# Hybrid decoder step: w_out in hi/lo products, output projection, norm and routing as one stage, one-hot rows for the first item

## The chip, the cores and the metric

The kernel runs on one core of a Trainium2 chip. The metric is the device time of one execution in microseconds; less is better. The profiler gives one execution with the times of every instruction, counted from the start of its span.

## The reference

One layer of a decoder is computed for 512 prompt tokens and 64 sample tokens (T = 576), of width 1024. Two branches (a Mamba-2 scan and a latent attention) are merged; what follows is the part that the change touches:

```
merged = sigmoid(g_a) * y_a + sigmoid(g_b) * y_b
out = merged @ p['w_out']
...
h = layer_norm(ALPHA * u + out)
logits = (h @ router_w + router_b)            # 32 experts
top_v, top_i = lax.top_k(logits, 4)
gate = softmax(top_v)
# each token's row goes to its 4 experts:
gu = xb @ w_gu[e] + b_gu[e]                   # (1024, 2048)
hidden = (clip(u) + 1.0) * (g * sigmoid(1.702 * g))
y = hidden @ w_dn[e] + b_dn[e]                # (1024, 1024)
out = layer_norm(ALPHA * h + sum over k of gate_k * y_k)
```

All is float32. Each expert's weights are 12 MB, and all 32 are read.

## The kernel before

The program is a row of stages. Each has its own block for every engine, its own semaphores, and ends in a barrier of all engines. The last four are the merge of branch a, `stage_out`, `stage_route` and `stage_experts_combine`. Tokens lie in NT = 5 tiles of 128 rows (the last has 64). KD = 8 is the number of 128-wide pieces of the width.

`stage_out` loads w_out (4 MB), the residual rows and the norm's gains, and multiplies in plain float32: for each tile 2 halves of 512 columns times 8 pieces (L1610), 80 matmuls; the profile has two records for each plain float32 matmul, so 160. VectorE (DVE) adds the residual and takes the statistics tile by tile (L1624 to L1634), then takes one root for all tiles, and only then scales all tiles (L1643 to L1647). SP stores the rows to `h_rows` in DRAM.

`stage_route` turns the rows on the tensor engine (PE, L1762), multiplies them by the router's weights (L1769), picks the four experts of a token on DVE (L1811 to L1834), counts with matmuls by a triangle of ones where in its expert's list each token stands (L1776 to L1779), and makes slot numbers and gates (L1847 to L1858). Then GpSimd (POOL) scatters 20 times 128 pairs of 8 bytes (token, row of the result) to the table `slots` in DRAM (L1750); when all have landed, SP and ScalarE (ACT) read the table back to `tok`: one transfer for the 32 experts and 18 for possible overflow items, 9 on each queue, each with its address loaded from SBUF (L1724, L1728, L1798). Meanwhile SP has loaded the first four weight slots of expert 0 (L1719).

`stage_experts_combine` works in items, one for each expert (E = 32) and more only where an expert has over 128 tokens. An item has NW = 12 weight slots of 1 MB, 8 for the gate and up matrix and 4 for the down matrix. A slot is loaded by SP to one of NRAW = 8 raw buffers (L1961), ACT rounds it to float32r (`w_hi`, L2123), DVE subtracts to get the rest (`w_lo`, L2172), and PE makes three products, hi times hi, hi times lo and lo times hi (`products`, L2044): 12 matmuls of 512 columns for a slot. `w_hi` and `w_lo` have four buffers (NHI). SP issues the load of a slot when the low part of the slot 8 before it is done (`wait_low`). POOL gathers the next item's rows of `h_rows` by an indirect DMA (L2002), copies the expert's column for the bias (L2006) and scatters the item's result to `y_rows` (L2016). PE turns the gathered rows in the middle of the down products (L2038, 8 turns for the rows, after 4 for the hidden part). Ahead of the first item there is a start: the gather of item 0's rows, four high and four low parts, the turns.

Each engine's instructions run in the order in which they are written for that engine; the only other order is by the semaphores.

## Time and profile before

| | us |
|---|---|
| median of 3 runs | 2855.95 (2853.38 to 2858.27) |
| the profiled execution | 2858.25 |
| its span | 2856.5 |
| granted tensor clock, mean | 0.935 |
| end of the last work of branch a's merge (DVE) | 1433.2 |
| first product with w_out | 1447.3 |
| first product of item 0 | 1641.6 |
| PE busy in all | 2562.5 (90%) |
| DVE busy in all | 1801.7 (63%) |

A row of the timeline reads: start, duration, engine, line, operation, what is written <- what is read, how many (xN), and in brackets how long the engine was idle before it and who ended that. The duration of a merged row runs from its first start to its last end. PE is the matmul, PEld the weight load that lies beside it, SPq, ACTq and POOLq are the engines' issuing sides.

### The profile page before, as it was taken

The numbers are of one execution on the slowest core, as the hardware profiler recorded it, in microseconds if no ns is written. First come the engines' busy times: TensorE is split into PE (matmuls) and PEld (weight loads), VectorE is DVE, ScalarE is ACT, GpSimd is POOL, SyncE is SP. The second block draws the span as 40 slices with busy tenths as digits, with TensorE's granted clock in tenths as the row PEclk, the third lists the DMA queues.
The fourth block names the chain that finished last, engine by engine and source line by source line (L and its number), as shares of the span: only waits on it lengthen the run. The fifth ranks groups of instructions, "written<-read, shape, count | busy, mean of one in ns | idle before, by whom it ended". The sixth has DMA issues, their size and how long they took to land. (4 is left out here: it accounts for less than half of the span.)

```text
span 2856.5 us, 35192 instructions
## 1 busy us (share of the span) xinstructions
PE 2562.5 (90%) x12631; PEld 1912.8 (67%) x12631; DVE 1801.7 (63%) x2118; ACT 1344.1 (47%) x1396; POOL 472.1 (17%) x333
## 2 busy tenths in 40 slices
PE   8697999698996999979976199999999999999996
PEld 5355555498994444548834188888888888888882
DVE  0343444333775666631013489999999999999996
ACT  0242322132324445420001177777777777777771
POOL 0002122000002233300001412222222222222220
PEclk9798999798998999979986599999999999999998
DMA  3103344132214313232123199999999999999995
GB/s 88 62 1 131 123 157 163 34 89 65 89 45 141 120 56 98 69 107 67 37 107 108 24 410 399 381 381 380 380 381 379 381 380 381 382 379 378 380 342 188
DMA packets 247096, 590.05 MB, mean 207 GB/s; under 512 B 28064, under 2 KB 117344, under 8 KB 242528
## 3 DMA queue, kind: packets, MB, share of 16 engines
q1 hardware_dynamic: 228392, 512.16, 49.6%
q0 software_dynamic: 17312, 76.57, 7.2%
q8 instruction: 64, 1.05, 0.2%
q14 instruction: 32, 0.26, 0.0%
q10 hardware_dynamic: 1296, 0.01, 0.0%
HBM read 555.78 MB, written 32.78 MB: 206 GB/s over the span
## 5 line engine op out<-in xcount | busy, mean ns | idle before, releaser
L2172 DVE TENSOR_TENSOR w_lo<-w_raw,w_hi 128x2048 fp32r<-128x2048 f32 x290 | 660.6, 2296 | 67.0 <-ACT w_hi L2123 66.6
L2123 ACT ACTIVATE w_hi<-w_raw 128x2048 fp32r<-128x2048 f32 x290 | 554.2, 1916 | 108.7 <-PE banks L2044 108.5
L2044 PE MATMUL banks<-w_hi,x_hi 128*128 128x512 f32 x1024 | 319.3, 393 | 5.1 <-DVE x_lo L2176 5.1
L2044 PE MATMUL banks<-w_hi,x_lo 128*128 128x512 f32 x1024 | 316.4, 390 | 0.0
L2044 PE MATMUL banks<-w_lo,x_hi 128*128 128x512 f32 x1024 | 316.0, 390 | 0.0
L2172 DVE TENSOR_TENSOR w_lo<-mergedT,w_hi 128x2048 fp32r<-128x2048 f32 x98 | 223.6, 2288 | 45.9 <-ACT w_hi L2123 45.9
L2123 ACT ACTIVATE w_hi<-mergedT 128x2048 fp32r<-128x2048 f32 x98 | 187.6, 1915 | 97.7 <-SPq L1971 62.7
L2044 PEld LDWEIGHTS banks<-w_lo,x_hi 128*128 128x128 f32 x1024 | 192.5, 188 | 40.6
L2044 PEld LDWEIGHTS banks<-w_hi,x_lo 128*128 128x128 f32 x1024 | 192.5, 188 | 40.4
L2044 PEld LDWEIGHTS banks<-w_hi,x_hi 128*128 128x128 f32 x1024 | 190.3, 188 | 43.4 <-issue 5.5
L2016 POOL DMA_INDIRECT y_rows<-xT,to_row x33 | 50.6, 1533 | 866.1 <-ACT xT L2153 865.8
L2044 PE MATMUL banks<-w_hi,h_lo 128*128 128x512 f32 x512 | 158.2, 390 | 0.0
L2044 PE MATMUL banks<-w_lo,h_hi 128*128 128x512 f32 x512 | 158.0, 390 | 0.0
L2044 PE MATMUL banks<-w_hi,h_hi 128*128 128x512 f32 x512 | 158.0, 390 | 0.0
L1306 PE MATMUL banks<-wz,xT 128*128 128x512 f32 (+1 forms) x320 | 145.1, 607 | 1.0 <-ACT zs L1421 1.0
L912 PE MATMUL banks_a<-xbcT,w_br_a 128*128 128x288 f32 x512 | 125.5, 406 | 0.0
L2038 PE MATMUL banks<-const,xT 128*128 128x128 f32 x520 | 68.3, 275 | 57.8 <-DMA xT<-h_rows,from_row 57.8
L912 PEld LDWEIGHTS banks_a<-xbcT,w_br_a 128*128 128x128 f32 x512 | 96.8, 190 | 26.1
L2044 PEld LDWEIGHTS banks<-w_hi,h_hi 128*128 128x128 f32 x512 | 96.1, 188 | 20.6
L2044 PEld LDWEIGHTS banks<-w_hi,h_lo 128*128 128x128 f32 x512 | 96.1, 188 | 20.3
L2044 PEld LDWEIGHTS banks<-w_lo,h_hi 128*128 128x128 f32 x512 | 96.1, 188 | 20.3
L1306 PEld LDWEIGHTS banks<-wz,xT 128*128 128x128 f32 (+1 forms) x320 | 57.6, 185 | 74.7 <-issue 74.3
(416 smaller groups left out, 4500.8 us busy)
## 6 DMA issues: line engine op xcount, KB each, us to landing
w_raw<-in_exp_w_gu SPq DMA_DIRECT2D x194, 1024.0 KB, 7.7
w_raw<-in_exp_w_down SPq DMA_DIRECT2D x96, 1024.0 KB, 8.2
mergedT<-in_exp_w_gu SPq DMA_DIRECT2D x66, 1024.0 KB, 8.4
mergedT<-in_exp_w_down SPq DMA_DIRECT2D x32, 1024.0 KB, 5.5
w_x<-in_w_in SPq DMA_DIRECT2D x12, 1024.0 KB
out<-h SPq DMA_DIRECT2D x20, 512.0 KB, 2.6
wz<-in_w_in SPq DMA_DIRECT2D x4, 2048.0 KB
dec<-acs_rows SPq DMA_DIRECT2D x16, 512.0 KB, 3.9
```

What stands on the lines that cost most here:

```text
L912: mm = pe.matmul(banks[:, b + 2 + piece, 0:H2], w_br[:, m % 2, k, :], x_of(k)[:, piece * H2:(piece + 1) * H2], start=(k == 0), stop=(k == ...
L1306: mm = pe.matmul(banks[0:n, 7, :], sb.xT[:, q, P * i:P * i + n], wz[:, g % 2, q, :], start=(q == 0), stop=(q == KD - 1))
L2016: pool.indirect_dma_start(out=io.y_rows, out_offset=bass.IndirectOffsetOnAxis(ap=to_row[:, par, :].bitcast(U32), axis=0), in_=y_out, in_of ...
L2038: mm = pe.transpose(banks[:, TURN_BANK[unit], k * P:(k + 1) * P], src[:, (k0 + k) * P:(k0 + k + 1) * P], K[:, K_ID:K_ID + P])
L2044: mm = pe.matmul(banks[:, bank + c, :], x[:, k, :], part[:, s % NHI, j, c * 512:(c + 1) * 512], start=start, stop=last)
L2123: act.activation(w_hi[:, s % NHI], raw(s, par), ACT.Copy).then_inc(hi_ready, 1)
L2172: dve.tensor_tensor(w_lo[:, s % NHI], raw(s, par), w_hi[:, s % NHI].bitcast(F32), ALU.subtract).then_inc(lo_ready, 1)
```

## The change

`stage_out` and `stage_route` become one stage, `stage_choose`, and some of the routing's DMA work moves into the experts' stage. Constants and buffers follow (`w_hi`, `w_lo`, `x_hi`, `x_lo`, `h_hi`, `h_lo` and `pair` now live across both stages; the raw buffers 0 to 5 are the separate ones and 6 and 7 the room of `mergedT`).

- w_out is loaded in four quarters, each split by ACT and DVE as an expert's slot is, and so is each tile of the merged input. PE makes three products for each pair: 5 tiles x 8 pieces x 3 x 2 halves = 240 matmuls.
- Each tile is normed in full before the next; PE turns tile i - 1 and makes its logits between the products of tile i.
- The ranks need 5 matmuls in place of 15, the counts 5 small ones with experts on the partitions; the list of overflow items comes from small matmuls in place of scans on one partition.
- For the first LISTED = 3 experts DVE makes one-hot tiles (`spot`). With those of expert 0 PE multiplies the rows themselves (40 plain float32 matmuls of 128 columns), which gives item 0's rows already turned. `tok` of the experts 0 to 2 comes from 15 matmuls of 2 columns.
- Slots 0 to 3 of expert 0 are split to their high parts within the stage, slot 0 to its low part too.
- The 20 scatters, the table's read and the 18 reads for overflow items move to the experts' stage: POOL scatters after it has issued the gather of item 1; SP reads the table after the loads of items 0 and 1, all 19 transfers on its own queue; POOL waits for them before the loop over the items from 2 on.

```diff
-            def _(pe):
-                pe.wait_ge(w_in_, 32)
-                for i in range(NT):
...
-                        for k in range(KD):
-                            mm = pe.matmul(banks[0:n, 2 * (i % 4) + c, :], sb.mergedT[:, k, P * i:P * i + n], w[:, c, k, :],
-                                           start=(k == 0), stop=(k == KD - 1))
...
+                for q in range(4):
+                    sp.dma_start(w_raw[q], io.wo[2 * P * q:2 * P * (q + 1), :].rearrange("(c p) n -> p c n", p=P)).then_inc(w_in_[q], 16)
...
                 for s in range(AHEAD):
-                    sp.dma_start(sb.w_raw[s], weight_slot(io, 0, s)).then_inc(first_in, 16)
-
-                sp.wait_ge(scattered, 16 * NT * TOPK)
...
+                    sp.wait_ge(wo_low, s + 1)
+                    sp.dma_start(w_raw[s], weight_slot(io, 0, s)).then_inc(first_in[s], 16)
...
+                def mix(i, q):
+                    n = ROWS[i]
+                    hi, lo = part_of(i)
+                    for j in range(2):
+                        k = 2 * q + j
+                        for x, part in ((hi, w_hi), (hi, w_lo), (lo, w_hi)):
+                            for c in range(2):
+                                mm = pe.matmul(banks[0:n, 2 * (i % 2) + c, :], x[:, k, 0:n], part[:, q, j, c * 512:(c + 1) * 512],
...
+                for i in range(NT):
+                    pe.wait_ge(m_low, i + 1)
+                    if i >= 2:
+                        pe.wait_ge(summed, i - 1)
+                    for q in range(4):
+                        if i == 0:
+                            pe.wait_ge(wo_low, q + 1)
+                        mm = mix(i, q)
+                        if q == 3:
+                            mm.then_inc(mixed, 1)
+                        if q == 2 and i >= 1:
+                            turn(i - 1)
...
+                    if i >= 1:
+                        logits(i - 1)
+                turn(NT - 1)
+                logits(NT - 1)
...
+                pe.wait_ge(spotted, 1)
+                for k in range(KD):
+                    for i in range(NT):
+                        n = ROWS[i]
+                        mm = pe.matmul(banks[:, k // 4, (k % 4) * P:(k % 4 + 1) * P], h[0:n, i, k * P:(k + 1) * P], spots[0:n, 0, i, :],
+                                       start=(i == 0), stop=(i == NT - 1))
...
+                pe.wait_ge(spotted, LISTED)
+                for e in range(LISTED):
+                    for i in range(NT):
+                        n = ROWS[i]
+                        mm = pe.matmul(banks[:, 2, 2 * e:2 * e + 2], spots[0:n, e, i, :], vals[0:n, i, e, :], start=(i == 0), stop=(i == NT - 1))
+                mm.then_inc(told, 1)
...
                 for s in range(AHEAD):
                     sp.sem_inc(w_in_[s], 16)
-                sp.wait_ge(x_in, 16)
-                n_more = items(sp, run)
+                run(0, 0)
+                run(1, 1)
+                sp.wait_ge(scattered, 16 * NT * TOPK)
+                with nc.allow_non_contiguous_dma(reason="a table of 8-byte pairs"):
+                    sp.dma_start(sb.tok[:, LISTED:E, :], io.slots.rearrange("(e c) a -> c e a", c=CAP)[0:P, LISTED:E]).then_inc(tabled, 16)
+                for q in range(NOVF + 1):
+                    at = sp.value_load(sb.item_slot[0:1, q:q + 1], min_val=0, max_val=E * CAP - P)
+                    sp.dma_start(sb.tok[:, E + q, :], io.slots[bass.ds(at, P), :]).then_inc(tabled, 16)
+                n_more = items(sp, run, 1)
...
-                gather(0, 0)
                 choose(0, 0)
                 pool.tensor_copy(to_row[:, 1, :], K[:, K_PAIR:K_PAIR + 1]).then_inc(to_put, 1)
                 pool.wait_ge(to_put, 1)
                 send(1)
-                n = items(pool, run)
+                e_next = expert(pool, 1)
+                gather(1, 1)
+                choose(e_next, 1)
+                for i in range(NT):
+                    n = ROWS[i]
+                    for k in range(TOPK):
+                        pool.indirect_dma_start(out=io.slots, out_offset=bass.IndirectOffsetOnAxis(ap=sb.slot[0:n, i, k:k + 1].bitcast(U32), axis=0),
+                                                in_=sb.pair[0:n, i * TOPK + k, :], in_offset=None).then_inc(scattered, 16)
+                scatter(0, 0)
+                run(1, 1)
+                pool.wait_ge(tabled, 16 * (NOVF + 2))
+                n = items(pool, run, 1)
```

On POOL, from the end of the routing into the items, this stood in a row before (`ISA` rows are register and semaphore work; x20 are the scatters):

```order
L1743 TENSOR_TENSOR b_all<-xT,b_all 32x3072
L1750 DMA slots<-pair,slot 20480x2 x20
L1707 UNCONDITIONAL_BRANCH
L140 ISA
L1994 UNCONDITIONAL_BRANCH
L1997 COPY from_row<-tok 128x1
L2002 DMA xT<-h_rows,from_row 128x1024
L2006 CAST pick<-const 128x128
L2027 CAST to_row<-const 128x1
L2016 DMA y_rows<-xT,to_row 2305x1024
```

and this stands there now (the changed kernel's own line numbers: L2129 is the scatter of pairs, L2096 the gather of rows, L2110 the scatter of results):

```order
L2120 CAST to_row<-const 128x1
L2110 DMA y_rows<-xT,to_row 2305x1024
L2038 TENSOR_LOAD item_expert
L2038 ISA x2
L2092 COPY from_row<-tok 128x1
L2096 DMA xT<-h_rows,from_row 128x1024
L2100 ISA
L2100 COPY pick<-const 128x128
L2129 DMA slots<-pair,slot 20480x2 x20
L2103 COPY to_row<-tok 128x1
L2110 DMA y_rows<-xT,to_row 2305x1024
L2038 TENSOR_LOAD item_expert
```

The gather of item 0's rows is gone, that of item 1's rows stands ahead of the 20 scatters, and item 0's result and the gather of item 2's rows (the next L2096) stand behind them.

On PE, between the last logits and the first product of item 0, this stood before (L1776 and L1777 are the ranks, L1779 the counts):

```order
L1769 MATMUL banks<-wr,hT 64x32 x8
L1777 MATMUL banks<-sel,const 128x32
...
L1779 MATMUL banks<-sel,const 128x32 x5
L1707 UNCONDITIONAL_BRANCH
L2033 UNCONDITIONAL_BRANCH
L2038 MATMUL banks<-const,xT 128x128 x8
L1931 UNCONDITIONAL_BRANCH
```

and this stands there now (L1731 and L1733 are the ranks, L1736 the counts, L1743 the rows of item 0 by one-hot tiles, L1756 the list of overflow items, L1762 the `tok` of three experts):

```order
L1708 MATMUL banks<-wr,mergedT 64x32 x8
L1731 MATMUL banks<-mergedT,const 128x160
...
L1733 MATMUL banks<-mergedT,const 128x32
L1736 MATMUL banks<-const,mergedT 32x2 x5
L1743 MATMUL banks<-w_raw,h 128x128 x15
L1749 MATMUL banks<-over,const 32x2
L1750 MATMUL banks<-over,const 1x2
L1743 MATMUL banks<-w_raw,h 128x128 x20
L1756 MATMUL banks<-xT,const 1x18 x8
L1743 MATMUL banks<-w_raw,h 128x128 x5
L1762 MATMUL banks<-vals,w_raw 128x2 x15
```

The one-hot products take the place of the turns of gathered rows, and stand ahead of the barrier between the stages.

## Rows read from the trace of the kernel before

**Rows 1.** Busy time by stretch, from the end of branch a's merge to item 0.

```profile
core 0: us, PE busy (x) PEld busy (x) DVE busy (x) ACT busy (x) POOL busy (x), PEclk, DMA share, GB/s
1434.00:1447.30 13.30, 0.04 (x1) 0.04 (x1) 0.07 (x1) 1.25 (x1) 0.00 (x0) 0.59 0.95 343
1447.30:1519.40 72.10, 72.10 (x160) 29.61 (x160) 11.12 (x20) 0.00 (x0) 0.00 (x0) 0.96 0.12 43
1519.40:1585.30 65.90, 28.95 (x160) 28.22 (x160) 32.87 (x89) 9.81 (x14) 12.99 (x5) 0.54 0.34 116
1585.30:1629.20 43.90, 0.00 (x0) 0.00 (x0) 13.43 (x10) 0.00 (x0) 23.13 (x21) 0.50 0.09 2
1629.20:1641.60 12.40, 1.97 (x8) 1.57 (x8) 10.19 (x6) 8.28 (x6) 10.37 (x7) 0.50 0.44 113
```

**Rows 2.** Transfers from 1434 to 1642: GB/s in 40 slices of 5.2 us.

```profile
GB/s 267 389 402 329 79 0 0 0 0 0 0 0 3 2 0 0 0 36 165 192 60 131 332 406 154 0 0 0 0 0 1 1 1 1 0 8 3 0 101 181
```

**Rows 3.** The chain of work that ended last: pieces of items 0 and 1.

```profile
1641.64 12.53 PE banks L2044 x48
...
1670.55 1.31 PE banks L2038 x12
...
1672.33 17.71 PE banks L2044 x78
...
1706.41 1.31 PE banks L2038 x12
```

**Rows 4.** Busy time by stretch: the first products of item 0.

```profile
1641.60:1644.40 2.80, 2.76 (x7) 2.21 (x8) 0.00 (x0) 0.46 (x1) 0.98 (x3) 0.50 0.92 354
```

**Rows 5.** Timeline: plain float32 matmul records of 32 and 128 columns.

```profile
30.28 1.92 PE L239 MATMUL banks<-w_dt,xT 128*128 128x32 f32 x16
...
246.91 1.06 PE L430 MATMUL banks<-probT,val 128*128 128x128 f32 x8
...
1550.24 13.74 PE L1769 MATMUL banks<-wr,hT 128*128 128x32 f32 x80
```

**Rows 6.** Timeline of DVE: the norm, then the choice of experts.

```profile
1519.43 1.28 DVE L1624 SCALAR_TENSOR_TENSOR h<-x_tok,banks 64x512 f32<-64x512 f32 x2 [11.03 <-PE banks L1610]
...
1522.96 0.81 DVE L1643 TENSOR_SCALAR h<-h,mv 128x1024 f32<-128x1024 f32 x1
...
1538.02 1.22 DVE L1647 TENSOR_TENSOR h<-h,b_b 64x1024 f32<-64x1024 f32 x1
...
1564.13 0.57 DVE L1816 TENSOR_TENSOR lg<-banks,br 128x32 f32<-128x32 f32 x5 [20.89 <-PE banks L1769]
...
1568.53 0.09 DVE L1834 MEMSET sel<- 64x32 f32 x1
```

**Rows 7.** Costliest groups of the page: a slot's low and high part.

```profile
L2172 DVE TENSOR_TENSOR w_lo<-w_raw,w_hi 128x2048 fp32r<-128x2048 f32 x290 | 660.6, 2296 | 67.0 <-ACT w_hi L2123 66.6
L2123 ACT ACTIVATE w_hi<-w_raw 128x2048 fp32r<-128x2048 f32 x290 | 554.2, 1916 | 108.7 <-PE banks L2044 108.5
```

**Rows 8.** Timeline: scatters of pairs on POOL beside work of DVE.

```profile
1588.23 2.55 DVE L1869 TENSOR_TENSOR found<-match,code 1x2304 f32<-1x2304 f32 x1
1589.35 2.27 POOL L1750 DMA_INDIRECT slots<-pair,slot  x1 [0.30 <-issue]
1590.82 2.54 DVE L1870 TENSOR_REDUCE listed<-found 1x18 f32<-1x2304 f32 x1
1591.93 0.96 POOL L1750 DMA_INDIRECT slots<-pair,slot  x1 [0.30 <-issue]
```

**Rows 9.** Timeline: a gather of rows on POOL in an item.

```profile
1687.09 2.67 POOL L2002 DMA_INDIRECT xT<-h_rows,from_row  x1 [0.89 <-POOL from_row L1997]
```

**Rows 10.** Indirect transfers of the items, 1650 to 2750: time to landing.

```profile
DMA to landing us min/median/max: 7.7/8.7/9.6
```

**Rows 11.** Timeline: half of the reads for overflow items, on SP's queue.

```profile
1616.85 10.03 SPq L1728 DMA_DIRECT2D tok<-slots  x9
```

**Rows 12.** Busy time by stretch: the transfers in items 0 and 1.

```profile
1650.00:1700.00 50.00, 50.00 (x232) 41.52 (x231) 46.14 (x32) 38.09 (x28) 8.24 (x5) 1.00 1.03 410
```

More of the change, by code:

```diff
@@ L1927, in wait_low, with items @@
             eng.wait_ge(lo_ready, it * NW + (NW + s + 1))
[L1929 to L1931 removed]
+        def items(eng, body, first=0):
+            with eng.Fori(first, E // 2) as i:
                 body(i * 2, 0)
```

529 lines of the change are left out of this document (287 added, 242 removed).

## The prediction

> **What bounds the kernel now.** I read the chain of waits first. From item 0 on it is the tensor engine (PE) without a break: products of one item after the other, 35.86 us an item (the turns of gathered rows start at 1670.55 in item 0 and at 1706.41 in item 1), 17.71 us for 78 products, so 0.227 us for one of 512 columns [rows 3]. The page's share (PE 90% busy) is thus an average of two things. The 32 items are bound by PE, and the change alters nothing within a steady item. The 207.6 us between branch a's merge and item 0 are bound by waits: read by stretch, PE works 103 of them [rows 1]. It waits 13.3 us for w_out, has 72.1 us of products, then 65.9 us in which norm, turns, router and choice follow each other with 29 us of PE work, then 43.9 us with none (20 scatters, then the table's read), then 12.4 us of start for item 0. The question is when item 0's first product comes (1641.64 before), and what the work moved into the items costs them.
>
> **w_out.** Removed: 80 plain float32 matmuls, 72.1 us at a mean granted clock of 0.96 [rows 1]. Added: 240 products at 0.227, 54.5 us with the clock high. They start when the first quarter is there and split. The slices give 267 GB/s for the first 5.2 us, then some 390 [rows 2]: 1.05 MB by 4.3 us at the earliest, if the quarters land one by one; if they land together it is 13.3. I take 1440. The split is an expert slot's: high part 1.92, low part 2.29 [rows 7], so PE starts at 1444.3. The four quarters and two tiles of the input need 4 x 2.29 and about 2 x 1.2 of DVE (half a slot each, an estimate), 11.6 us from 1441.9, so the last low part ends at 1453.5. PE's first products are at the low clock, 0.50 granted (1.2 GHz), 0.40 us each [rows 4]. The old stage had a mean of 0.96 over 72.1 us [rows 1], which is 5.8 us at 0.5 and the rest at 1; I take the same 5.6 us, 14 low products and 34 high ones: 1444.3 + 5.6 + 7.7 = 1457.6. Take 1458 for the end of tile 0, 1455 to 1461 as bounds.
>
> **Tiles 1 to 4.** 4 x 48 x 0.227 = 43.6. Turns: the chain's piece of 12 takes 1.31 [rows 3], so 8 take 0.87, four times 3.5. Logits: 16 records of 32 columns take about 1.76 us at the high clock (to the next row's start; the row says 1.92) [rows 5], three times 5.3. A tile's PE work is then 13.6 us, and a tile's norm on DVE is 3.5 to the scaling [rows 6] and 3.3 for the scaling (1522.96 to 1539.2 for five tiles), 6.8, plus 1.2 for the next tile's low part. So the norm of tile i ends ahead of the turn that PE makes 8.2 us after it; it hides behind the products, and would cost 1 us for each 1 us by which it passed 8.2. With 0.3 for each small wait: 1458 + 43.6 + 3.5 + 5.3 + 1.1 = 1511.5. The last tile has no cover: norm 6.8, 8 turns and the copies about 1.3, 16 logit records at the low clock 0.17 each (13.74 for 80) [rows 5] 2.7. Logits are there at 1522.3, where before it was 1564.1.
>
> **Choice, ranks, one-hot.** From the first add to the selection 4.5 us [rows 6], now 4.7: 1527.0. Ranks: 480 columns in all; plain float32 of 512 columns takes 72.1 / 80 = 0.9 at the high level, so 480 at the low one 1.7, with loads 2.0. Two copies and five one-hot tiles, 1.4: 1530.4. The rows of item 0 are 40 plain matmuls of 128 columns, 80 records. The nearest row has 8 in 1.06, 0.113 apart at the high level [rows 5], so 9.0; at the low level twice as much, 18. PE did almost nothing from 1518 on, so it starts low, and these matmuls are dense, so I expect the high level after some 5 us: 11.5. Small matmuls between them 1, then 30 records of the token table at 0.11 to 0.17 [rows 5], 4.2, and 0.4 for DVE's last copies: 1547.6. DVE's own list (overflow list, slots, gates, low part of the rows) is some 14 us from 1533 by the old stage's ops of 0.3 and ends about then. Barrier about 0.9, and PE's first instruction 0.3 later: **first product at 1548.8**, 92.8 us earlier. Gone with it are the 20 scatters, the table's read and item 0's gather, parts and turns, that is the whole 43.9 and 12.4 us of waiting [rows 1]; late next is the chain above.
>
> **What moves into the items.** Call the stage's start S. PE starts at S + 0.3, so it reaches the turns of item 2's rows (in item 1) 64.8 us later by the old distance 1706.41 - 1641.64 [rows 3]: S + 65. *POOL*: bias column, the dummy result and the gather of item 1 keep it to about S + 10.5. Then come the 20 scatters, and behind them in its queue item 0's result and the gather of item 2. A scatter takes 0.96 beside a reduction of DVE and 2.27 beside a subtraction or product of two tiles, where it ends with DVE's instruction plus 0.9 [rows 8]; a gather in an item takes 2.67 [rows 9]. With 0.3 between, 20 take 25 us with DVE idle and 59 us at 2.97 each. DVE has 12 long subtractions in 35.86 us and shorter work between, so I take 2.3: S + 56.5. Item 0's result and the next gather need some 7 more, landing 8.7 [rows 10]: item 2's rows land near S + 71, 6 us late. At 1.27 a scatter it would be S + 51, no wait; at 2.97, S + 85, 20 late.
>
> The Trainium skill (GPSIMD Engine Reference, Key points) says that GpSimd shares its SBUF interfaces with VectorE and contends with DVE instructions that have two SBUF inputs. By that rule every scatter behind a low part is slow and the sum has its loss; if it did not hold in an item, the result would be that of rival A. This trace agrees: 2.27 against 0.96 us.
>
> *SP*: the loads of item 2's slots 4 to 11 stand behind the wait for the scatters and 19 table transfers. Nine took 10.03 [rows 11], so the 19 take about 21 us. SP can reach the wait when the low part of item 1's slot 7 is done, S + 56; the scatters have landed at about S + 60. The queue is free at S + 82, the load lands 5 to 8 us later, its parts need 4.2 [rows 7]: ready at S + 92 to 94. PE needs that slot (number 28) at S + 3.6 + 28 x 2.99 = S + 87.3, or S + 93.3 after the 6 us already lost. So the two waits overlap, and the second adds 0 to 1. The pause is survivable since eight buffers and the backlog carry PE; afterwards transfers run at 410 GB/s [rows 12] against the 380 that 13.6 MB in 35.86 us need, so the lead returns. An idle PE restarts at the low clock, 0.50 granted [rows 4], some 1 us more. Sum: **7 us lost** once, bounds 0 and 25. One more place is tight: slot 4 is issued at S + 0.3, lands by S + 8 if it takes the 7.7 of [rows 10], and is split by S + 13.5, with a table load on ACT; PE needs it at S + 15.6. I count this as nothing lost; if it lands 3 us later it costs 1.
>
> **Sum.** 2856.5 - 92.8 + 7 = 2770.7 of span. The profiled execution has 1.75 us outside its span and is 2.3 above the median, so 2770.7 + 1.75 - 2.3 = 2770.
>
> **Rivals.** *A, no loss in the items*: scatters near 1.3 us, or the gather lands in time. For it: short work of DVE leaves gaps. Against it: rows 8 and 9. 2763. *B, a long loss in items 1 and 2*: scatters near 3 us, so that SP starts its table reads at S + 75 and slot 28 is ready at S + 109, 22 late, or the small transfers wait behind the weights' backlog. For it: the gather's 2.67 and a queue that is full. 2780 to 2800. *C, the new stage is longer*: quarters that land together (PE starts at 1451, 7 later), the one-hot products low all through (7 more), the norm past its cover. 2771 to 2785. *D, slower than before*: item 2's rows come so late behind the scatters on POOL that the loss passes the 92.8 us. Rows land at about S + 10.5 + 20 t + 14; against S + 65 this is a loss of 20 t - 40, so t must pass 6.6 us a scatter. The longest here is 2.67, so it needs small indirect transfers that block POOL behind the weights, which only an item's load would show. At t = 7 it gives 2863. *E, the products gain nothing*: if PE stayed at the low clock in the mixed stream of tiles, the 192 products of tiles 1 to 4 cost 0.40 and 33 us more: 2803. Against it: 0.96 granted in the old products [rows 1]; the short logits between should not undo it.
>
> **How the numbers follow.** Forecast 0.45, A 0.15, B 0.20, C 0.13, E 0.04, D 0.02, the stage shorter than I sum 0.01. The predicted time is the forecast's, 2770. Below, A with a stage 8 us shorter gives 2755; above, B and C up to 2792; what lies outside is most of E, D and the far end of B. Measurement can tell about 0.2% (6 us) from no change. Every case but D and a bit of its neighbourhood ends faster by more: faster 0.97, same 0.01, slower 0.02.
>
> **What would show it.** In the changed profile: the first w_out product between 1442 and 1447; the tiles' products 0.227 each at a granted clock near 1; PE idle for under 1 us at each turn; logits complete near 1522; the first product of item 0 near 1549; items of 35.86 us but for one; 20 scatters in about 46 us, each ending just after a low part; a PE wait for gathered rows in item 1 of some 6 us; SP's 19 reads near S + 60 to S + 82. It is wrong if item 0 starts past 1560, if PE waits again after item 2, or if a steady item is longer than 35.9 us.

## The result, and the profile after

| | before | after |
|---|---|---|
| median (lowest to highest) | 2854.66 us (2852.06 to 2858.27), 4 runs | 2806.22 us (2800.5 to 2809.62), 4 runs |
| profiled execution, span | 2856.5 us | 2801.1 us (2803.2 with what lies around it) |
| granted clock, mean | 0.935 | 0.945 |

The ratio is 0.983, 95% interval 0.9818 to 0.9842: 1.7% faster. The prediction of 2770 us, range 2755 to 2792, is 36 us too low, and the time lies above the range. Of these 36 us, 29 are in one term, the loss within the first items, and 2 in a first product of item 0 that comes later. The other 5 are between executions: the sum took the profiled one to be 2.3 us above the median, and it is 3.0 below.

Busy time by stretch of the changed kernel, the same columns as in [rows 1]: the wait for w_out, the five tiles, the rest of the routing stage, the 56 us from item 0's first product, and the gap in item 2.

```profile
1431.30:1441.30 10.00, 0.00 (x0) 0.00 (x0) 3.52 (x2) 4.75 (x3) 0.67 (x2) 0.66 0.82 314
1441.30:1510.40 69.10, 67.05 (x320) 53.57 (x321) 43.25 (x44) 16.66 (x21) 13.93 (x3) 0.95 0.49 172
1510.40:1550.50 40.10, 27.00 (x191) 24.02 (x189) 27.15 (x89) 11.09 (x11) 0.42 (x2) 0.70 0.03 7
1550.50:1606.50 56.00, 47.61 (x192) 37.85 (x193) 40.37 (x26) 31.36 (x23) 41.57 (x27) 0.91 0.96 300
1648.10:1668.80 20.70, 0.08 (x2) 0.04 (x1) 2.29 (x1) 4.95 (x3) 1.61 (x4) 0.62 0.57 193
```

The stage did what was said: 119 us from the merge's end to item 0, where it was 208 before, and PE (TensorE) starts item 0 at 1550.54 (forecast 1548.8). What went wrong is in the last two lines. In [rows 12] the weights move at 410 GB/s and PE is busy all the time; here the mean is 300 and PE is idle for 8.4 of 56 us, and it idles 20.6 us more in item 2.

The chain that ended last shows both places (start, us, what):

```profile
1556.34 27.85 DMA w_raw<-in_exp_w_down
1584.29 1.92 ACT w_hi L2225
...
1590.51 1.92 PE banks L2142 x12
...
1618.24 2.50 SPq L2064
...
1621.49 13.77 SPq L2067
...
1656.09 7.00 DMA w_raw<-in_exp_w_gu
1663.18 1.28 ACT L2225
1664.47 1.92 ACT w_hi L2225
1666.41 2.30 DVE w_lo L2272
1668.76 6.30 PE banks L2148 x17
```

In [rows 3] the same chain is PE alone. Here it leaves PE twice. First to a load of weights that took 27.85 us to land. Then to SP: L2064 is the read of the table, L2067 the 18 reads of the overflow lists; after them the next load of weights leaves at 1656.09, lands in 7.0 us, and needs ACT's function table (the load at L2225), the high part and the low part (5.5 us) before PE has a product again.

How much was lost is read from the turns of the gathered rows, L2142 x12, against item 0's first product. Before, they stand 28.9 us behind it, and one item is 35.86 us [rows 3]. After, they stand at 39.97, 77.5 and 136.6 us. The excess, called the loss from here on, is 11.1 us in item 0, 12.7 by item 1 and 36.0 by item 2; from there on each item takes 35.86 again. The span adds up: 1550.54 + 36.0 + 1214.6 for the rest, and in the kernel before 1641.64 + 1214.9. Forecast was a loss of 7 where 36.0 came; the other steps of the span together are within 2 us. So the experiments ask what these 36.0 us are.

### The profile page after: what moved, and what is told of

The parts are those of the page before. It is cut to its first block and busy times, and to the rows that moved or that the text cites. A ratio compares the mean times of both kernels' runs of the same rounds, so it can differ in the third digit from the quotient of the medians.

```text
span 2801.1 us, 35520 instructions
## 1 busy us (share of the span) xinstructions
PE 2560.0 (91%) x12813; PEld 1931.8 (69%) x12813; DVE 1813.2 (65%) x2130; ACT 1358.1 (48%) x1409; POOL 474.1 (17%) x331
## 5 line engine op out<-in xcount | busy, mean ns | idle before, releaser
L2225 ACT ACTIVATE w_hi<-w_raw 128x2048 fp32r<-128x2048 f32 x288 | 550.4, 1916 | 113.5 <-PE banks L2148 104.0
L2148 PE MATMUL banks<-w_hi,x_hi 128*128 128x512 f32 x1024 | 321.2, 395 | 23.9 <-DVE w_lo L2272 21.6
L2225 ACT ACTIVATE w_hi<-mergedT 128x2048 fp32r<-128x2048 f32 x96 | 184.1, 1917 | 41.0 <-PE banks L2148 34.5
L2110 POOL DMA_INDIRECT y_rows<-xT,to_row x33 | 50.8, 1538 | 847.1 <-ACT xT L2255 846.7
L963 DVE TENSOR_TENSOR prod_a<-banks_a,sig_a 128x576 f32<-128x576 f32 x8 | 6.1, 757 | 154.2 <-PE banks_a L918 154.2
```

What stands on the lines that cost most here:

```text
L963: dve.tensor_tensor(o.rearrange("p (a n) -> p a n", a=2), banks[:, b + 2:b + 4, 0:H2], sig[:, m % 2, :].rearrange("p (a n) -> p a n", a=2) ...
L2110: pool.indirect_dma_start(out=io.y_rows, out_offset=bass.IndirectOffsetOnAxis(ap=to_row[:, par, :].bitcast(U32), axis=0), in_=y_out, in_of ...
L2148: mm = pe.matmul(banks[:, bank + c, :], x[:, k, :], part[:, s % NHI, j, c * 512:(c + 1) * 512], start=start, stop=last)
L2225: act.activation(w_hi[:, s % NHI], raw(s, par), ACT.Copy).then_inc(hi_ready, 1)
```

## The experiments

The first w_out product comes between 1436.6 and 1449.1 us, by differences in earlier stages that no edit touches. So the table has distances within one execution: the stage from the first w_out product to item 0's first product, and the loss up to the turns of items 0, 1, 2 and 3 (after item 3 it stays). In two places the turns of the rows themselves waited, e4 in item 3 and e11 in item 1; there the table has what was lost once they were through. The times, beside the kernel before on the same chip, are of one profiled execution each for e1 to e8. The four to five executions that e9, e10 and e11 have lie up to 17 us apart, so these single times are rough; the argument rests on the distances, and those are of one execution each too. The stage differs by up to 5 us between runs whose edits hardly touch it (107.8 in e7, 112.9 in e3), so a difference of that size in it proves nothing.

| run | stage | item 0 | 1 | 2 | 3 | time (before) |
|---|---|---|---|---|---|---|
| after | 109.2 | 11.1 | 12.7 | 36.0 | 36.0 | 2806.2 (2854.7) |
| e1 scatters early | 129.0 | 4.8 | 4.8 | 24.6 | 24.6 | 2808.2 (2855.3) |
| e2 half of them | 114.7 | 7.1 | 7.2 | 27.3 | 27.3 | 2799.7 (2855.3) |
| e3 place-first lists | 112.9 | 5.7 | 5.7 | 14.9 | 14.9 | 2790.9 (2855.3) |
| e4 reads on POOL | 110.2 | 9.3 | 12.0 | 12.0 | 21.6 | 2791.7 (2855.3) |
| e5 stride of 648 | 109.5 | 10.1 | 12.7 | 35.8 | 35.8 | 2811.4 (2860.9) |
| e6 slot 4 early | 110.3 | 4.5 | 11.9 | 35.2 | 35.2 | 2810.5 (2860.9) |
| e7 no list reads | 107.8 | 11.0 | 12.7 | 13.6 | 13.6 | 2783.7 (2860.9) |
| e8 plain products | 132.3 | 12.2 | 13.8 | 35.3 | 35.3 | 2824.1 (2860.9) |
| e9 = e3 + e7 | 109.5 | 6.2 | 6.2 | 6.2 | 6.2 | 2778.6 (2860.7) |
| e10 = e9 and three more | 109.7 | 2.5 | 2.5 | 2.5 | 2.5 | 2772.4 (2860.7) |
| e11 = e10 less one edit | 105.4 | 1.6 | 3.8 | 3.8 | 3.8 | 2775.0 (2863.3) |

### e1 and e2: the scatters out of item 0

```diff
                 pool.wait_ge(b_low, 2)
+                pool.wait_ge(noted, 2)
+                pool.wait_ge(cleared, 16)
+                for u in range(0, 20):
+                    i, k = divmod(u, TOPK)
+                    n = ROWS[i]
+                    pool.indirect_dma_start(out=io.slots, out_offset=bass.IndirectOffsetOnAxis(ap=sb.slot[0:n, i, k:k + 1].bitcast(U32), axis=0),
+                                            in_=sb.pair[0:n, i * TOPK + k, :], in_offset=None).then_inc(scattered, 16)
+                pool.wait_ge(scattered, 16 * 20)
```

This stands at the end of POOL's part of the routing stage, and the same 20 are gone from item 0. In e2 the range ends at 10.

> The 20 scatters of slot pairs are issued and waited for at the end of the routing stage, so the items hold none; nothing else is moved. The figure to read is the distance from item 0's first product to the turns of the gathered rows (39.97 us in the changed kernel, 28.91 in the kernel before), and the same to item 2's turns (136.6, before 100.6). Theory 1 (each scatter of 128 pairs of 8 bytes takes some 0.55 us of all 16 DMA engines from the weights, 11 us for 20): item 0 falls back to 29 to 31 us, and the weights move at 400 GB/s and more from 1.5 item-slots on. Rival 1 (item 0 is late because the loads of slots 4 and up start 6.5 us later against the products than before, and the scatters only pass through gaps): item 0 stays at 38 to 40. The loss around item 2 (25 us) should stay in both, 20 to 27 us, as SP's table reads are untouched. The whole kernel is not expected to gain: the routing stage grows by the 20 scatters, some 20 to 30 us, and at least 11 come back.

> Ten of the 20 scatters go to the end of the routing stage and are waited for there, ten stay in item 0. Theory 1 (0.55 us of transfer per scatter): item 0 takes 33 to 36 us to the turns, midway between 28.9 and 40. If there is a slack that the first scatters use up (the products are not waiting at first), it is nearer to 30. Rival 1 (late start of the loads): 38 to 40, as with all 20 or with none. Item 2's loss stays at 20 to 27 us.

Item 0 took 33.67 us to the turns with no scatter (a loss of 4.8), 36.05 with ten (7.1), 39.97 with twenty (11.1). Neither theory alone has it: the scatters are worth 6.3 us, and 4.8 are there without them. What these 4.8 are, ACT (ScalarE) shows in e1, by its timeline:

```profile
1574.14 1.28 ACT L2227 ACT_TABLE_LOAD   x1 [34.31 <-DMA w_raw<-in_exp_w_gu]
1575.44 1.92 ACT L2227 ACTIVATE w_hi<-w_raw 128x2048 fp32r<-128x2048 f32 x1
1578.73 1.92 ACT L2227 ACTIVATE w_hi<-w_raw 128x2048 fp32r<-128x2048 f32 x1 [1.38 <-DMA w_raw<-in_exp_w_gu]
1581.76 1.92 ACT L2227 ACTIVATE w_hi<-mergedT 128x2048 fp32r<-128x2048 f32 x1 [1.11 <-DMA mergedT<-in_exp_w_gu]
```

Each of the first high parts waits for its load. The loads of slots 4 and up leave 1.0 us after item 0's first product; in the kernel before they left at 1636.18, 5.5 us ahead of it, since its item 0 had its own rows to turn first. And they start slowly; why is not shown. GB/s in 40 slices of 1.4 us from the first product on, of before, after and e1:

```profile
GB/s 287 421 421 418 421 418 415 413 418 398 404 398 413 410 415 392 413 418 415 392 413 418 415 398 407 418 415 392 410 404 418 401 407 415 421 421 413 410 401 415
...
GB/s 12 76 234 222 170 395 421 418 424 408 417 226 64 123 255 411 411 298 120 381 405 99 296 387 296 279 155 281 396 416 413 184 252 401 323 284 401 407 418 421
...
GB/s 12 64 217 190 199 386 421 418 421 421 415 407 415 413 410 407 410 415 398 413 410 410 410 407 413 415 404 407 415 395 407 410 407 415 407 410 410 421 418 418
```

In after and e1 alike the first five slices have 12 to 234 GB/s. The holes (64, 120, 99, 155) are in after alone, while the scatters run, and in e1 they are gone.

### e3: another layout of the lists

```diff
-    c[:, K_BASE:K_BASE + E] = CAP * np.arange(E)
+    c[:, K_BASE:K_BASE + E] = np.arange(E)
-    dve.tensor_tensor(place, rank, K[:, K_BASE:K_BASE + E].unsqueeze(1).broadcast_to((P, NT, E)), ALU.add)
+    dve.scalar_tensor_tensor(out=place, in0=rank, scalar=float(E), in1=K[:, K_BASE:K_BASE + E].unsqueeze(1).broadcast_to((P, NT, E)), op0=ALU.mult, op1=ALU.add)
-    sp.dma_start(sb.tok[:, LISTED:E, :], io.slots.rearrange("(e c) a -> c e a", c=CAP)[0:P, LISTED:E])
+    sp.dma_start(sb.tok[:, LISTED:E, :], io.slots[0:E * P].rearrange("(c e) a -> c e a", e=E)[:, LISTED:E])
```

The overflow codes, and the reads that use them, follow the layout. So the edit changes three things at once: where the scatters write, the shape of the table's read, and the 18 reads, which now take every 32nd pair.

> The list in DRAM is laid out by place first and expert second, so that the table read takes 128 pieces of 232 bytes in place of 3712 pieces of 8 bytes; the 18 small reads stay with 128 pieces each. Theory 2 (the first small read's issue was blocked 13.8 us because the 3712 pieces stand behind the weights' backlog and fill the queue): the block is gone, all 18 reads go out at 1.1 us, SP's pause falls from 37.9 to 21 to 24 us, and the loss around item 2 from 25 to 8 to 12 us; the kernel is 13 to 17 us faster than the changed one, 2789 to 2793. Rival 2 (a small read's issue waits for the backlog of the weights whatever the table's shape): a block of 10 us or more remains, the pause is 32 or more, and the kernel gains 5 us at most.

SP's queue by its timeline, after first, then e3:

```profile
1618.24 2.50 SPq L2064 DMA_DIRECT2D tok<-slots  x1
1621.49 32.92 SPq L2067 DMA_DIRECT2D tok<-slots  x18
1656.09 1.06 SPq L2049 DMA_DIRECT2D w_raw<-in_exp_w_gu  x2
```

```profile
1618.40 0.47 SPq L2064 DMA_DIRECT2D tok<-slots  x1
1619.61 20.53 SPq L2068 DMA_DIRECT2D tok<-slots  x18
1641.82 1.06 SPq L2049 DMA_DIRECT2D w_raw<-in_exp_w_gu  x2
```

The backlog of weights is much the same in both, about 12 us at full rate, and SP comes to the table at about the same time. With 3712 pieces the first small read is held for 13.77 us; with 128 it is not, and SP's pause falls from 37.9 to 23.4 us, the loss after item 1 from 23.3 to 9.2. So the backlog alone does not block. Nor do the pieces alone: the kernel before read its whole table, 4096 pieces of 8 bytes, with no weights under way, and the reads behind it went out at 1.1 us each.

```profile
1615.37 0.37 SPq L1724 DMA_DIRECT2D tok<-slots  x1
1616.85 10.03 SPq L1728 DMA_DIRECT2D tok<-slots  x9
```

It takes both, many pieces behind a backlog. The Trainium skill (DMA: Bandwidth & Descriptors, Rules for kernel authors) says that a last dimension that is strided is lowered to one descriptor per element, and should be rearranged to be contiguous. The case here is a neighbour of that one, since the last dimension is a contiguous pair of 8 bytes in a strided list. No run shows the elements of a pair apart; what the runs show is the price at the next instruction of the queue.

What I had not expected is item 0: its loss fell to 5.7, though the same 20 scatters of 8-byte pairs run there. Packets of the 56 us from the first product, after and then e3:

```profile
DMA packets 4991, 16.80 MB, mean 300 GB/s; under 512 B 902, under 2 KB 902, under 8 KB 4987
...
DMA packets 5998, 20.68 MB, mean 369 GB/s; under 512 B 963, under 2 KB 963, under 8 KB 5994
```

The number of small packets is about the same (902 and 963), and the bytes, nearly all of them weights, are almost a quarter more. In this stretch neither kernel has read the table yet, so only the places of the scatters differ. So it is not the count of small writes that costs, but where they go.

### e4: the list reads on POOL

```diff
-                for q in range(NOVF + 1):
-                    at = sp.value_load(sb.item_slot[0:1, q:q + 1], min_val=0, max_val=E * CAP - P)
-                    sp.dma_start(sb.tok[:, E + q, :], io.slots[bass.ds(at, P), :]).then_inc(tabled, 16)
...
                 run(1, 1)
+                run(2, 0)
+                for q in range(NOVF + 1):
+                    at = pool.value_load(sb.item_slot[0:1, q:q + 1], min_val=0, max_val=E * CAP - P)
+                    pool.dma_start(sb.tok[:, E + q, :], io.slots[bass.ds(at, P), :]).then_inc(tabled_late, 16)
+                run(3, 1)
```

> SP does the table read alone; the 18 reads of the overflow lists go to POOL's queue, after item 2's result. Theory 2: the load that follows the table read on SP takes over the block of some 14 us, SP's pause is 14 to 18 us in place of 37.9, which the lead of the buffers covers but for 0 to 5 us; 20 to 25 us come back and the kernel is at 2781 to 2788. Rival 2b (it is the sum of the reads that matters, wherever they run: their 2304 pieces of 8 bytes cost the weights as the scatters do): some 10 us are lost again in item 2 or 3, and the gain is 12 to 16 us. Item 0 stays at 39 to 41 us in both.

The block moved to SP's loads, as theory 2 says: two loads take 13.05 us from 1622.40, and item 2 loses nothing. But item 3 lost 9.6 us, 8.2 of them without work and the rest at slower turns and products behind it. POOL (GpSimd) and PE by their timelines:

```profile
1679.87 1.30 POOL L2134 DMA_DIRECT2D tok<-slots  x2
...
1699.46 0.53 POOL L2134 DMA_DIRECT2D tok<-slots  x1 [0.61 <-issue]
```

```profile
1710.53 1.97 PE L2145 MATMUL banks<-const,xT 128*128 128x128 f32 x8 [8.16 <-DMA xT<-h_rows,from_row]
```

```profile
DMA packets 4703, 15.87 MB, mean 397 GB/s; under 512 B 835, under 2 KB 835, under 8 KB 4702
```

The last row is of 1675 to 1715: the weights were hardly slowed (a mean of 397 GB/s; 373 to 398 in most slices while the reads ran, 406 to 418 in most of those before and after), so rival 2b's mechanism is out too, although its size was near. The gather of item 4's rows stood behind 18 reads of 1.14 us in POOL's queue. It is the wait that the prediction put in item 1, for another instruction. These small reads take little from the stream, where the scattered small writes of the changed kernel took a fifth. But each of them reads 128 neighbouring pairs, so the comparison does not tell reads from writes.

### e5: a stride of 648 places

```diff
-CAP = 640
+CAP = 648
```

> The lists keep their expert-first layout, but an expert's part is 648 places long in place of 640, so the same 8-byte pairs go to addresses 5184 bytes apart in place of 5120. Theory 1a (the scatters are cheap when an address pattern suits the memory; 5120 bytes apart is a bad one): item 0 loses 5 to 7 us as with the place-first layout, in place of 9 to 11, and the weights' rate during the scatters stays near 370 GB/s. Rival 1b (what helped the place-first layout is that a scatter's 128 pairs fall into one stretch of 4 KB, not 32 stretches): item 0 loses 9 to 11 as in the changed kernel, at a mean near 300 GB/s. Item 2's loss stays at 22 to 26.

A loss of 10.1 in item 0, and a mean of 305 GB/s over the same 56 us:

```profile
DMA packets 5063, 17.07 MB, mean 305 GB/s; under 512 B 908, under 2 KB 908, under 8 KB 5059
```

The exact distance of the lists is not it. What is left is that the place-first layout puts a scatter's pairs into a few KB that lie together, and the expert-first one into 32 stretches. That this is the cause is an inference from two layouts; no run varied it in steps.

### e6: slot 4 loaded early

```diff
                     sp.dma_start(io.h_rows[P * i:P * i + ROWS[i], :], h[0:ROWS[i], i, :]).then_inc(stored, 16)
+                sp.dma_start(w_raw[4], weight_slot(io, 0, 4)).then_inc(early, 16)
...
-                run(0, 0)
+                run(0, 0, AHEAD + 1)
```

> The load of item 0's slot 4 is moved to the routing stage, behind the rows' stores, where its buffer is free once the gains are used; all else as in the changed kernel. By the late start of the loads (items begin with loads 1 us behind the first product, where before they began 5.5 us ahead), one slot fewer to fetch is 2.6 us at 400 GB/s, and the slow first 5 us of a restarted stream stay: item 0's loss goes from 9 to 11 down to 6.5 to 8.5 us. Rival (item 0 is set by the scatters alone, which hold back slots 8 to 11 whatever came first): no change, 9 to 11. Item 2's loss stays at 22 to 26.

Item 0's loss fell to 4.5, more than the load is worth, but item 1's grew to 7.4: 11.9 in all against 12.7. Neither expectation had this. PE waits only when the stream is behind; one slot fewer in item 0 puts off the debt that the scatters make, and does not remove it. With scatters that cost little it should come to its worth (e10, e11).

### e7: no list reads

```diff
+                n_reads = sp.value_load(sb.n_over[0:1, 0:1], min_val=0, max_val=NOVF)
+                with sp.If(0 < n_reads):
                     for q in range(NOVF + 1):
                         at = sp.value_load(sb.item_slot[0:1, q:q + 1], min_val=0, max_val=E * CAP - P)
                         sp.dma_start(sb.tok[:, E + q, :], io.slots[bass.ds(at, P), :]).then_inc(tabled, 16)
```

POOL waits for them under the same condition, and the places of absent items are filled with a valid row in the routing stage.

> The 18 reads of the overflow lists run only where an expert has more than 128 tokens, which none has in this data; so they are not executed. The table read of 3712 pieces stays. Theory 2 (the loss around item 2 is SP's pause, of it 14 us behind the backlog of weights and table pieces, 19 to 20 in 17 more reads): the first load after the table read is blocked 12 to 14 us, the pause is 14 to 17 in place of 37.9, and the loss from item 1 on falls from 25 to 2 to 5 us; unlike with the reads on POOL nothing is lost later. Whole kernel: 20 to 23 us faster than the changed one, 2782 to 2787. Rival (it is the block, not the reads, that starves the products): the loss stays over 12.

```profile
1619.64 1.70 SPq L2065 DMA_DIRECT2D tok<-slots  x1
1624.15 12.15 SPq L2050 DMA_DIRECT2D w_raw<-in_exp_w_gu  x2
1636.56 1.07 SPq L2050 DMA_DIRECT2D mergedT<-in_exp_w_gu  x2
```

```profile
1666.28 1.53 PE L2148 MATMUL banks<-const,xT 128*128 128x128 f32 x12 [0.76 <-DVE xT L2291]
```

The loads are blocked as in e4, yet item 2 loses only 0.9 us where it lost 23.3. The three pauses of SP stand in a row: 16.9 us cost 0.9 (the block alone), 23.4 cost 9.2 (the reads alone, e3), 37.9 cost 23.3 (both). The pause less its cost is 16.0, 14.2 and 14.6 us. So the buffers' lead covers some 14 to 16 us, and what a pause has beyond that is lost in full. The reads alone starve PE, the block alone all but doesn't, and together they cost more than the sum of the two.

### e8: plain products in the new stage

```diff
-                    hi, lo = part_of(i)
                     for j in range(2):
                         k = 2 * q + j
-                        for x, part in ((hi, w_hi), (hi, w_lo), (lo, w_hi)):
-                            for c in range(2):
-                                mm = pe.matmul(banks[0:n, 2 * (i % 2) + c, :], x[:, k, 0:n], part[:, q, j, c * 512:(c + 1) * 512],
-                                               start=(k == 0 and x is hi and part is w_hi), stop=(k == KD - 1 and x is lo))
+                        for c in range(2):
+                            mm = pe.matmul(banks[0:n, 2 * (i % 2) + c, :], sb.mergedT[:, k, P * i:P * i + n], w_raw[q][:, j, c * 512:(c + 1) * 512],
+                                           start=(k == 0), stop=(k == KD - 1))
...
-                    sp.wait_ge(wo_low, s + 1)
+                    sp.wait_ge(mixed, NT)
```

> In the new stage the products of w_out are plain float32, 80 matmuls as before, straight from the raw tiles; the splits on ScalarE and VectorE still run, unused, and item 0's first slots are loaded once the last tile is mixed. It tells what the hi/lo products are worth inside the new stage. By the prediction's terms (72.1 us for 80 plain products against 54.5 for 240 at 0.227, and the first 5 us at the low clock in both) the stage from the first w_out product to item 0's first product takes 15 to 20 us more than the changed kernel's 109.2, 124 to 129, since the norm stays hidden in both. Rival (with the longer products the norms, turns and clock losses between tiles shrink, or the tail hides part): 8 to 13 us more. The losses in items 0 and 2 stay.

```profile
1442.60:1523.70 81.10, 81.10 (x241) 38.41 (x241) 43.35 (x44) 16.57 (x21) 13.03 (x3) 0.96 0.22 68
1523.70:1574.90 51.20, 32.49 (x192) 28.80 (x191) 27.29 (x89) 11.09 (x11) 0.43 (x3) 0.60 0.35 129
```

The stage is 23.1 us longer, above both expectations: 12.0 in the tiles, 11.1 behind them. Of the 11.1, 5.6 are there before the last logits are read, and these are of my edit's making. The high part of the first expert's slot stands ahead of the last tile's root on ACT, and its load now leaves only after the last product:

```profile
L1775 ACT ACTIVATE w_hi<-w_raw 128x2048 fp32r<-128x2048 f32 x4 | 7.6, 1903 | 10.4 <-DMA w_raw<-in_exp_w_gu 10.4
```

The other 5.5 are PE's work, 32.5 us in place of 27.0 at a mean granted clock of 0.60 and not 0.70. So the hi/lo products are worth 12.0 us in the tiles, not the 17.6 (72.1 less 54.5) of bare products, and with them the loads are free to leave early. Some of the difference is tile 0's wait for its gains, which the longer products hide and the shorter ones don't: in e10, where the wait is gone, the tiles take 65.3 us, 15.8 less than here.

### e9, e10 and e11: versions that beat both

e9 has the layout of e3 and the condition of e7. e10 adds the early slot 4, and these two:

```diff
                 for i in range(NT):
-                    sp.dma_start(h[0:ROWS[i], i, :], token_dram(io.xp, io.xs, i)).then_inc(x_in, 16)
-                sp.dma_start(g_b, io.g1.broadcast_to((P, D))).then_inc(gb_in, 16)
-                sp.dma_start(b_b, io.b1.broadcast_to((P, D))).then_inc(gb_in, 16)
+                    sp.dma_start(h[0:ROWS[i], i, :], token_dram(io.xp, io.xs, i)).then_inc(x_in[i], 16)
+                    if i == 0:
+                        sp.dma_start(g_b, io.g1.broadcast_to((P, D))).then_inc(gb_in, 16)
+                        sp.dma_start(b_b, io.b1.broadcast_to((P, D))).then_inc(gb_in, 16)
...
+                for u in range(0, 8):
+                    i, k = divmod(u, TOPK)
+                    n = ROWS[i]
+                    pool.indirect_dma_start(out=io.slots, out_offset=bass.IndirectOffsetOnAxis(ap=sb.slot[0:n, i, k:k + 1].bitcast(U32), axis=0),
+                                            in_=sb.pair[0:n, i * TOPK + k, :], in_offset=None).then_inc(sb.scattered, 16)
```

The eight scatters stand where e1 has its 20, on a semaphore that both stages share, so that the routing stage doesn't wait for them. e11 leaves them out.

> The place-first layout of the lists (scatters into one stretch, table read of 128 pieces) together with the overflow reads that run only where there is overflow; none has it in this data, so they are not executed. If the two causes found add up, item 0 loses 5 to 6 us as in the run with the layout alone, item 1 nothing, and item 2 at most 1 us (9.2 with the layout and the reads, 0.9 with neither read nor layout): 5 to 7 us in all against 36 in the changed kernel, so 2775 to 2779. If instead the block of some 13 us at SP after the table read was the table's pieces and nothing else matters, it is the same figure; if the backlog of weights blocks SP anyway, a block stays at the next load but costs nothing, since the queue is then full of weights. A third loss at a new place (item 2 or 3, as with the reads on POOL) would show the sum is not what I think.

> As e9, and three more edits: slot 4 of item 0 is loaded in the routing stage; 8 of the 20 scatters are issued there while DVE still writes the gates and the one-hot products run (they are waited for with the others in item 1); and the gains and the first tile's input are fetched ahead of the other tiles' input, each tile waiting for its own, so that the norm of tile 0 does not wait 7.3 us. Theory: item 0 is short by its start of the loads and its 20 scatters; 2.6 us come from slot 4, 0 to 2 from the 8 scatters, so the loss is 1 to 4 us in place of 5 to 7. The routing stage is 1 to 4 us shorter by the norm of tile 0 and the clock it costs (2.0 us wait and one more stretch at the low clock). Together 2768 to 2775, ratio to the kernel before 0.970 to 0.973. Rival (the slow first 5 us of the stream after a pause is the whole of item 0's loss, whatever is to be fetched): loss 5 to 6, 2773 to 2778.

> As e10, with all 20 scatters in item 0 again; the layout, the reads only where there is overflow, the early slot 4 and the order of the gains stay. In e10 VectorE's last step of the routing stage came 4.1 us after the last product, while the early scatters ran, and item 0 lost 2.5 us. If the early scatters were what held up the end of the stage: the stage from the first w_out product to item 0's first product falls from 109.7 to 105 to 106 us, item 0's loss is 3 to 4 us, and the whole is 2766 to 2771 in fast chips, 2 to 4 us under e10. Rival (the delay in e10 was a chance of that execution, as no such delay stands in e1, which had scatters at the same place): the stage is 105 to 106 too, but the whole is not under e10's median, since only its profiled run was late and the 8 early scatters are worth 1 us.

| | median (lowest to highest), runs | ratio to before, 95% interval |
|---|---|---|
| e9 | 2778.62 (2771.13 to 2781.12), 4 | 0.972, 0.970 to 0.974 |
| e10 | 2772.4 (2770.15 to 2781.32), 5 | 0.9699, 0.9678 to 0.972 |
| e11 | 2775.01 (2770.19 to 2787.48), 4 | 0.971, 0.9685 to 0.9736 |

e9 is as expected: 6.2 us lost in item 0 and nothing later, so the two causes add up and no third place shows. e10 lost 2.5 us there, as expected. Its stage was not shorter, though. From the first w_out product to the last logits but one it took 65.3 us in place of 69.1, since the norm of tile 0 no longer waited for its gains, but the end came late. DVE (VectorE) in e10, then in e11:

```profile
1551.91 0.16 DVE L1972 CAST tok<-banks 128x3 int32<-128x3 f32 x1 [5.92 <-DMA dec<-acs_rows]
```

```profile
1546.34 0.16 DVE L1965 CAST tok<-banks 128x3 int32<-128x3 f32 x1 [2.85 <-PE banks L1766]
```

In e10 PE had finished 4.1 us before this copy; e11, without the early scatters, has no such delay, and its stage is 105.4. But e1 had scatters at the same place and its copy came at once, and e11's median is not under e10's. So what held that copy is open (the releaser named is a transfer of an earlier stage and can't be right). Against e9, the trace of e10 shows 3.7 us less loss, that of e11 2.4 us less loss and 4.0 us less stage; but the intervals of the three overlap, and the times do not tell them apart. All three are faster than both kernels.

In e11, slot 4 early and the place-first layout brought item 0's loss down to 1.6 us with all 20 scatters in it. Then PE was early enough to meet another wait, in item 1, for the gathered rows of item 2:

```profile
1617.62 1.09 PE L2152 MATMUL banks<-const,xT 128*128 128x128 f32 x8 [1.91 <-DMA xT<-h_rows,from_row]
```

POOL had issued that gather at 1608.72, behind the 20 scatters (1557.94 to 1602.45) and item 0's result.

## Why the prediction was wrong, point by point

**The new stage: right, in part by luck.** Terms and measured: first w_out product 1444.3 and 1441.3, end of tile 0 1458 and 1454, tiles' end 1511.5 and 1510.4, logits 1522.3 and 1520.5, start of the one-hot products 1530.4 and 1529.2, first product of item 0 1548.8 and 1550.54. Several errors nearly cancel. The first w_out product came 3.0 us earlier, 1.9 of them because the stage before ended earlier. The tiles then took 69.1 us and not 67.2, the one-hot products with the small ones between 14.7 and not 12.5, and what follows them 0.7 us more than taken. The restart at the low clock was foreseen, and it came again on the way. The norm of tile 0 waited for its gains (7.26 us, on DVE), which the prediction did not have. So PE waited 2.01 us for tile 0's rows, and then the granted clock fell to 0.50:

```profile
1456.64 1.22 DVE L1846 SCALAR_TENSOR_TENSOR h<-h,banks 128x1024 f32<-128x1024 f32 x1 [7.26 <-DMA w_raw<-in_ln_b]
...
1464.23 1.10 PE L1700 MATMUL banks<-const,h 128*128 128x128 f32 x8 [2.01 <-DVE h L1863]
...
1465.30:1468.50 3.20, 3.20 (x9) 2.46 (x8) 0.01 (x1) 0.71 (x2) 0.00 (x0) 0.50 1.02 408
```

**The scatters' interval: right in kind.** 20 in 37.8 us, one in 1.9 where 2.3 was taken: 0.96 us for some, 2.3 to 3.0 for others, as [rows 8] had it.

**The wait for item 2's rows: did not occur here.** The prediction took 6 us for the gather behind the scatters. The turns of that gather stand in item 1 without idle time:

```profile
1628.04 1.47 PE L2142 MATMUL banks<-const,xT 128*128 128x128 f32 x12
```

The scatters were done earlier than taken, and PE was late already by 11 us. The mechanism is real. In e11, where item 0 loses only 1.6 us, it stands at the place that the prediction named, with 1.91 us: the rows released PE 69.3 us after the stage's start, where 71 was taken. e4 has it in item 3, with 18 reads in place of 20 scatters, 8.16 us.

**"Slot 4 ... I count this as nothing lost": the first step that failed.** The load landed in 7.5 us, where 7.7 was taken, and the slot was ready 14.4 us after the stage's start. PE wanted it at 13.5 and waited 0.93 us. The prediction had this need at 15.6, too late by its own rows: the 48 products of slots 0 to 3 take 12.53 us [rows 3]. But slot 4 is the small part, and the term had no other. The slots behind it came slowly, at 12 to 234 GB/s for the first seven us, and then with holes. The loss is 4.8 us without any scatter (e1), 6.3 more with them. The sum had the indirect transfers as work of POOL alone. That small transfers and weights meet was named only in rivals B and D, as weights that hold up the small ones; here it is the small writes that hold up the weights. The row that spoke of the slow start was [rows 2]: in its last slice, when the items' loads have begun (they left at 1636.18), it has 181 GB/s. I used its first slice, 267, for w_out, and not its last one for item 0.

**SP's pause, 21 us: the term that was mis-sized most.** It was 37.9. The 18 reads took 1.09 us each as [rows 11] says, and SP reached the table at S + 68.0 in place of S + 60, by the loss of item 0. The other 14 are the block of the first small read. The prediction priced 19 transfers by nine that ran with nothing else in the queue. The pause was put down to cost 0 to 1 us beyond the rows' wait, and cost 23.3. Even the 21 us as taken would have cost more: by e3, e7 and the changed kernel the lead covers 14 to 16 us of a pause, so 5 to 7 would have been lost (an estimate). Rival B had "the small transfers wait behind the weights' backlog" at 0.20, and 2780 to 2800 for it. It was the right rival. With no loss at all the sum is 2763, so its upper end holds a loss of 37 us, as large as the one that came, though for a reason that explains 23.3 of it. That the median lies above 2800 even so is the 2 us of the stage and the 5 us between executions.

**Range.** The sum's own bounds for the loss were 0 and 25, and the range ended at 2792, which leaves out the upper part of B. It was built on one loss at a time. Both came, 12.7 and 23.3, and the larger part of them has one root: the change moves many tiny transfers from a stretch in which the queues were idle into the one stretch where 380 of 410 GB/s are in use. The 4.8 us of the late and slow start are there without it.

The Trainium skill (DMA: Bandwidth & Descriptors, Specifications) says that below 512 bytes a transfer makes the DMA engine read, modify and write. The holes in the changed kernel's stream agree in direction; but e3 has as many packets under 512 B and its stream is 23% faster, so size alone does not price them, and here the measurement decides.

## What to carry to other kernels

A step that is moved takes its transfers along: price each not by the idle stretch where it was measured, but by what the queue and the memory do where it will run, and count the pieces, since behind the same backlog 3712 pieces of 8 bytes held the next instruction of the queue for 14 us where 128 pieces of 232 bytes did not. This stretch ran at over 90% of its transfer rate and had no room for scattered small writes, and one buffer fetched earlier mostly moved that debt (e6). When buffers are to cover a pause, work out how long: here they covered 14 to 16 us, and every us beyond was lost in full, so that two pauses in a row cost more than each by itself.

## What the runs showed of the hardware

- 20 scatters of pairs of 8 bytes (128 in each, 64 in the last four) into 32 stretches took the weights' stream over 56 us from 376 GB/s (e1, with the same slow start and no scatter) to 300, with 1.4 us slices down to 64. Into one region of a few KB for each scatter it was 369. 18 reads of 128 neighbouring pairs left it at 397, against 406 to 418 beside them (e4).
- The experts' loads, when they start after a pause, move about 200 GB/s for some 5 us, then 415 to 421 (item 0 in the kernel before, in the changed one and in e1; again after SP's pause at 1656). The load of w_out does not: in the kernel before it leaves at 1433.96 and moves some 390 GB/s from 1436 on. What makes the difference is open.
- Behind a backlog of weights and 3712 pieces, SP's queue was held for 12 to 14 us at the next instructions (a read in the changed kernel, loads in e4 and e7). With the same backlog and 128 pieces it was not (e3), nor with 4096 pieces and no backlog (the kernel before).
- A pause of SP's loads cost PE what it had beyond 14 to 16 us: 0.9 of 16.9 (e7), 9.2 of 23.4 (e3), 23.3 of 37.9 (the changed kernel).
- PE waited 2.0 us for tile 0's rows, and its granted clock was then 0.50 for 3.2 us, though PE had been busy before it (1.00 granted) and was after it.
- A subtraction on DVE that takes 1.2 us elsewhere took 7.82 beside one of POOL of 7.47 us; it ended 1.1 us after POOL's. Nothing waited for it:

```profile
1476.40 7.82 DVE L1836 TENSOR_TENSOR h_lo<-mergedT,h_hi 128x1024 fp32r<-128x1024 f32 x1
```

```profile
1475.67 7.47 POOL L1676 TENSOR_TENSOR b_all<-xT,b_all 32x3072 fp32r<-32x3072 f32 x1 [10.72 <-ACT b_all L1810]
```
